# VectorE's order inside the delta pairs: convolution taps of v into its waits, masked attention ahead of level one

## What is computed

```python
qkv = silu(causal_dwconv(concatenate([dq, dk_, dv_]), dn_conv_w))      # 4 taps per channel
cq, ck = l2norm(cq), l2norm(ck)
G = cumsum(g);  L = where(causal, exp(G[:, None] - G[None, :]), 0)
A = where(strict, einsum('id,jd->ij', k_beta, kc) * L, 0)
sol = triangular_solve(eye + A, [v * beta, k_beta * exp(G)])           # u, w
attn = where(causal, einsum('id,jd->ij', qc, kc) * L, 0)
# then over the chunks:
v_new = u - w @ S;  o = q_dec @ S + attn @ v_new;  S = S * d + k_dec.T @ v_new
```

## Time and profile before

| | us |
|---|---|
| median of 3 runs | 2281.53 (2281.12 to 2284.86) |
| the profiled execution's own time | 2283.54 |
| its span | 2281.8 |
| TensorE busy, matmuls | 2227.6 (98%) |
| VectorE busy | 1076.5 (47%) |
| ScalarE busy | 801.2 (35%) |
| GpSimd busy | 943.0 (41%) |

### The profile page before, as it was taken

One profiled execution on the slowest core, in us unless ns is written; L12 is line 12 of the kernel. 1 busy time (PEld: TensorE's weight loads), 2 busy tenths in 40 slices (PEclk: granted clock), 3 DMA queues, 4 the chain that ended last, 5 costly groups with the idle time before them and its releaser, 6 DMA issues.

```text
span 2281.8 us, 30104 instructions
## 1 busy us (share of the span) xinstructions
PE 2227.6 (98%) x12106; PEld 1794.7 (79%) x12106; DVE 1076.5 (47%) x1508; ACT 801.2 (35%) x825; POOL 943.0 (41%) x509
## 2 busy tenths in 40 slices
PE   7999999999999999999999999999999999999998
PEld 6888888776656888888887888787878778888887
DVE  5423203775854343331063532646556545888801
ACT  4222213447644342222143532332424243322213
POOL 4555544343312445554443244323233343444344
PEclk9999999999999999999999999999999999999999
DMA  4233223343332333223232123212121243322232
GB/s 151 93 93 106 87 99 95 89 70 56 78 101 94 98 105 92 92 92 101 92 103 93 56 70 95 77 56 75 56 75 56 75 148 109 94 92 92 73 101 83
DMA packets 162169, 203.36 MB, mean 89 GB/s; under 512 B 12236, under 2 KB 117015, under 8 KB 162071
## 3 DMA queue, kind: packets, MB, share of 16 engines
q1 hardware_dynamic: 155296, 197.16, 28.5%
q10 hardware_dynamic: 6775, 4.80, 0.7%
HBM read 191.45 MB, written 10.49 MB: 88 GB/s over the span
## 4 chain that ended last, share of the span: by engine, by line
PE 83%; DVE 7%; issue 5%; ACT 3%; POOL 1%; DMA 0%; ACTq 0%; POOLq 0%; DVEq 0%
PE PS L213 23%; PE PS L215 22%; PE PS L214 22%; PE PS L244 2%; PE PS L246 2%; PE PS L245 2%; DVE cv L2350 2%; POOL wl L204 1%; PE PS L1134 1%; PE PS L2159 1%; PE PS L1674 1%; PE PS L1231 1%; PE PS L2176 1%; DVE work L2428 1%; PE PS L1050 0%
## 5 line engine op out<-in xcount | busy, mean ns | idle before, releaser
L204 POOL TENSOR_TENSOR wl<-raw,wh 128x1024 fp32r<-128x1024 f32 x335 | 864.0, 2594 | 1233.7 <-ACT wh L193 1195.9
L213 PE MATMUL PS<-h_hi,wh 128*128 128x512 f32 x1696 | 678.8, 400 | 7.9 <-ACT stage_a L863 3.0
L215 PE MATMUL PS<-h_hi,wl 128*128 128x512 f32 x1696 | 663.3, 391 | 0.0
L214 PE MATMUL PS<-h_lo,wh 128*128 128x512 f32 x1696 | 662.9, 391 | 0.0
L193 ACT ACTIVATE wh<-raw 128x2048 fp32r<-128x2048 f32 (+1 forms) x214 | 332.6, 1554 | 837.8 <-PE PS L215 791.7
L213 PEld LDWEIGHTS PS<-h_hi,wh 128*128 128x128 f32 x1696 | 319.5, 188 | 92.1 <-issue 20.3
L215 PEld LDWEIGHTS PS<-h_hi,wl 128*128 128x128 f32 x1696 | 319.6, 188 | 67.8
L214 PEld LDWEIGHTS PS<-h_lo,wh 128*128 128x128 f32 x1696 | 319.9, 189 | 61.8 <-issue 0.7
L213 PE MATMUL PS<-act_hi,wh 128*128 (+1 forms) x528 | 205.8, 390 | 1.0 <-POOL wl L204 1.0
L694 DVE SCALAR_TENSOR_TENSOR xT<-PS,xT 128x512 f32<-128x512 f32 x40 | 27.2, 689 | 379.6 <-PE PS L215 379.5
L214 PE MATMUL PS<-act_lo,wh 128*128 (+1 forms) x528 | 205.5, 389 | 0.0
(11 more groups left out here) (450 smaller groups left out, 2842.0 us busy)
## 6 DMA issues: line engine op xcount, KB each, us to landing
raw<-in_w_in_dram SPq DMA_DIRECT2D x94, 512.0 KB, 4.6
raw<-in_w_up_dram SPq DMA_DIRECT2D x82, 512.0 KB, 4.7
raw<-in_w_down_dram SPq DMA_DIRECT2D x132, 256.0 KB, 2.7
raw<-in_w_gate_dram SPq DMA_DIRECT2D x42, 512.0 KB, 3.9
raw<-in_w_in_dram SPq DMA_DIRECT2D x20, 256.0 KB, 3.7
raw<-in_w_out_dram SPq DMA_DIRECT2D x16, 256.0 KB, 2.9
raw<-in_w_ret_br_dram SPq DMA_DIRECT2D x8, 512.0 KB, 4.3
gates<-stage SPq DMA_DIRECT2D x16, 256.0 KB, 5.9
```

The source lines that it names most:

```text
L204: ins = nc.gpsimd.tensor_tensor(wl[:, slot, part], raw[:, slot, part], wh[:, slot, part].bitcast(F32), ALU.subtract)
L213: nc.tensor.matmul(dst, sh, mh, start=start, stop=False)
L214: nc.tensor.matmul(dst, sh, ml, start=False, stop=False)
L215: return nc.tensor.matmul(dst, sl, mh, start=False, stop=stop)
```

## The change

Only `delta_dve` changes. v's taps 0 and 1 go ahead of the wait for eR (behind a new wait for cin), tap 2 between the clipping and the product that makes A, tap 3 stays behind A. The factor `rk` goes ahead of the start blocks, the two instructions of the masked attention go from level one to right behind the start blocks, ahead of the memset and the scaled v. No instruction is added or removed, and the other engines' programs stay as they were.

```diff
                      "dve")
+            v_taps = conv_taps(dve, pp, 4, 6, cin)
+            await_point(dve, "act", pp, "cin")
+            v_taps[0]()
+            v_taps[1]()
             await_point(dve, "act", pp, "eR")
             dve_link(tt(chunks(wE), chunks(PS[:, 4:6, :]), per_head(Gn, pp), ALU.subtract))
             at_point(dve.tensor_scalar(wE, wE, 0.0, None, ALU.max), "dve")
+            v_taps[2]()
             await_point(dve, "pe", pp, "kk")
             await_point(dve, "act", pp, "eE")
...
-            v_taps = conv_taps(dve, pp, 4, 6, cin)
-            for tap in v_taps:
-                tap()
+            v_taps[3]()
+            await_point(dve, "act", pp, "rk")
+            rk3 = rk.rearrange("p (e c) -> p e c", e=2)
+            dve_link(tt(rk3, rk3, beta[:, :, 2 * pp:2 * pp + 2].rearrange("p c h -> p h c"), ALU.mult))
             start_block(Tc, wU, level[1], lambda r: r)
             await_point(dve, "act", pp, "AT")
             at_point(start_block(Uc, wAT[:, :, :], level1T, other), "dve")
+            dve_link(tt(tiles(wE), tiles(wE), everywhere(seen), ALU.mult))
+            tt(wE, PS[:, 0:2, :], wE, ALU.mult).then_inc(attn_set, 1)
             dve.memset(quarters(wU, 64, 0), 0.0)
-            await_point(dve, "act", pp, "rk")
-            rk3 = rk.rearrange("p (e c) -> p e c", e=2)
-            dve_link(tt(rk3, rk3, beta[:, :, 2 * pp:2 * pp + 2].rearrange("p c h -> p h c"), ALU.mult))
             scaled_v(dve, pp, 6)
...
-                if l == 0:
-                    dve_link(tt(tiles(wE), tiles(wE), everywhere(seen), ALU.mult))
-                    tt(wE, PS[:, 0:2, :], wE, ALU.mult).then_inc(attn_set, 1)
```

## The result

| | before | after |
|---|---|---|
| median | 2281.89 (2281.12 to 2284.86) | 2257.52 (2256.78 to 2259.0) |
| profiled execution, its span | 2283.54, 2281.8 | 2256.78, 2255.1 |
| mean granted clock | 0.992 | 0.998 |

The change is faster by 24.4 us between the medians; the ratio is 0.9892, 95% interval 0.9875 to 0.9909. That is 1.1% of the time, and the two sets of runs do not overlap. A second set on another occasion gave 2256.86 against 2281.57.

What follows compares the result with a forecast made beforehand. TensorE, its matmuls filling 98% of the span, was taken as the bound, so only its waits and half clock could be won. 3.6 + 3.05 = 6.65 a pair (6.95 with the race won); 6.75 x 4 = 27.0, giving 2254.5, range 2249 to 2265.

Steps and rivals of the forecast that it cites:

- Taps 0 and 1: VectorE's idle 3.09 before eR: the two taps, 2.35 together, fit in and cost nothing, with 0.7 left.
- Tap 2: Gap of 1.20 on VectorE before A: the tap needs 1.42, so A comes 0.24 later, +0.24.
- v's SiLU and GpSimd's weights: TensorE's waits ahead of level one: -0.47 from earlier SiLU, -0.62 from GpSimd's weights; X starts 0.85 earlier, at 1562.65.
- VectorE's chain to the first mask: VectorE's new order, with holds by GpSimd: first mask at 1564.3 against 1564.78 if GpSimd is first at the last add.
- Level one: Correction 0.65 after the mask, at 1564.95; second level's X at 1566.9 instead of 1570.48, 3.6 earlier.
- The prediction's sign of being wrong: A stretch at 0.50 clock remaining in each pair, or level one's masks starting 2 us after its X is there.
- Clock, -3.05: Granted clock 1.00 throughout: level two 2.1 shorter, level three 0.95, together -3.05 a pair; bounds 0 and 3.4.
- the race at the last add: VectorE's last add meets GpSimd's L204: second level's X 3.6 earlier if GpSimd is first, 3.9 if VectorE wins.
- Rival 1: Clock falls all the same, on level one's short gaps and small matmuls: saving 14.4 alone, 2267; chance 8%.
- Rival 2: One more GpSimd hold, 2.25, between tap 3 and level one's mask: mask at 1566.55, saving 17.6, 2264; chance 6%.
- Rival 3: Attention ahead of the first mask only shifts the stall from level two to level one, clock falling there: 2282; chance 2%.
- Rival 4: Taps slow by their form, 2.82 wherever they stand: A 5.9 late, clock falls, +9.3, 2291; chance 4%.

Runs made afterwards that it cites:

- The filled gap: Kernel before, with 24 matmuls that nothing needs put into TensorE's wait between level one's corrections and level two: 2271.49 us, ratio 0.9957.
- attention_alone: Kernel before, with only the masked attention moved, ahead of the memset; taps and factor in their old places: 2283.16 us, ratio 1.0008.
- factor_back: The change, with the 128x8 factor back in its old place behind the memset: 2257.41 us, ratio 0.9894.
- x_early: The change, with TensorE's wait for ScalarE's copy of the fourth gates' product moved from ahead of level one's X to behind it: 2257.84 us.
- mask_early: The change, with the masked attention's product with PSUM moved into level two and the memset into level three, behind the masks: 2257.38 us.
- factor_alone: Kernel before, with only the 128x8 factor moved, ahead of v's taps: 2263.03 us, ratio 0.9921.
- both_early: The change with X not waiting for ScalarE's copy and the PSUM product and memset moved behind later masks: 2254.82 us; second set 2254.58 against 2256.86.

## Why the prediction was right, and where it was off

The range and the side held: 2254.5 forecast, 2257.5 measured. Of the 3.0 between them 1.5 lie in the stage that the sum is about, 1.1 between the stage and the medians, and 0.4 in the median before (2281.53 of three runs then, 2281.89 of four now). By the prediction's own steps:

- **Taps 0 and 1 cost nothing**: right. They took 2.3 and left VectorE 0.92 idle before eR; 0.7 was said.
- **Tap 2, +0.24**: right. The wait for A went from 0.23 to 0.47.
- **v's SiLU and GpSimd's weights, -0.47 and -0.62**: both waits are gone, but X came only 0.88 earlier from A, where 1.09 was worked out (0.85 plus A's 0.24). Of the 0.21 missing, 0.17 is in v's transposes: with TensorE waiting ahead of them (before) their loads start within 0.82 from the first to the next matmul's, directly behind the product (after) 0.99. A wait that goes does not give back all of what it showed.
- **VectorE's chain to the first mask**: from A's transposes the prediction has T0 at +14.3 and the mask at 1564.3 - 1543.84 = +20.5; measured +14.4 (1547.55 + 2.87 - 1536.04) and +20.77. Each hold that the text names is there, in its order, and so is GpSimd's won race. This step bore the most reasoning and missed by 0.3: the PSUM product, the memset and the scaled v take 3.05 from the end of seen to the mask, where 2.79 was added up.
- **Level one**: X to X 4.19, 4.25 worked out, and here two errors cancel. The prediction let the correction follow the mask by 0.65, read from a level in which X and not the mask set the correction (1.97 behind X). Where the mask sets it, it follows in 0.47 (1556.81 to 1557.28). So the mask's 0.3 of lateness cost only 0.1. The prediction's sign of being wrong, masks 2 us behind X, was not far: they start 1.75 behind it.
- **Clock, -3.05**: levels two and three 2.13 and 0.83 shorter, 2.96 together, the second of them 0.12 less than the 0.95 said. That 0.95 was not what its own terms give: 0.78 for X and 0.1 for the matmuls behind it are 0.88. The filled gap gives 2.96 by itself.

Together 6.41 a pair by A to A (102.68 against 109.09, the third pair 102.79) against the 6.75 of the sum; over the stage 25.5, not 27.0. Of the 0.34 a pair that is missing, the start of X is 0.21, of which level one gave 0.06 back, the clock 0.09, and 0.1 was weight that the 6.75 put on VectorE winning the race at the last add, which it lost. The profiled executions differ by 26.8 only because 1.4 of it lies ahead of the first changed instruction (below). Against that the medians' 24.4 is 1.1 below the stage's own gain; 0.7 of it is that the profiled execution after was the fastest of its four. The outcome of the race at the last add, 0.05 us, was not something that the prediction could call; it had priced both.

Rival 1, the clock swinging on short gaps alone, is out: of the kernels tried, only `attention_alone`, which keeps the long gap, falls to half clock in the pairs; the others have the short gaps and 1.00. In the pairs, gaps of 0.36 to 1.5 never came with a fall, and gaps of 3.4 and 4.2 did in the traces kept. The Trainium skill (TensorE: Matmul & The Clock Gate, "A second HAM failure mode: psum-queue depth-cycling") tells of micro-idles between groups of matmuls that were frequent enough to make the clock swing, in another kernel, of bf16 matmuls with 512 columns; in this one the short gaps were not enough. The 3.4 may not lower the clock every time: of 35 runs of the kernel before that stand beside these experiments and the result, four took 2276.1 to 2279.1 at a mean clock of 0.994 to 0.995. At 2.96 us for each stretch at half clock that would be one or two of them missing (an estimate; no trace of such a run was kept). Rival 2, one more hold ahead of the mask, did not come: TensorE waited 0.25 longer for the mask than its shortest gap, not the 2.6 of that case (its mask at 1566.55 and 0.65 behind it, against 1564.62). Rival 3, the gap that moves whole, is what `attention_alone` measures, with the taps and the factor left in their old places. Rival 4 fell with the taps at 0.75 in every form.

What the prediction did not see, though its rows held it, is how little of the change was needed. It read the stall as attention standing in the wrong level. But 2.1 of the 3.33 of seen was time held by GpSimd's operation (unheld it takes 1.22), in a race lost by 0.11 us. Once VectorE waits for level one's X and not the other way round, seen starts 0.4 earlier against GpSimd and wins, and two quite different edits reach that: the change with the attention taken back (2259.3), or one 128x8 instruction moved (2263.0). The gap fell from 3.42 to 0.89 and the half clock went with it, on an order of arrival. Beside the kernel before, the factor alone gave 18.5, taps and factor 22.8, all three moves 24.4; given the taps and the attention's new place, the factor's place gave nothing (`factor_back`). No run moves the taps alone.

## What to carry to other kernels

Where VectorE instructions with two SBUF operands come out two or four times as long as the same form elsewhere, look at GpSimd's timeline before looking at the instruction: what is priced may be GpSimd's operation. Here the 128x8 instruction paid 2.2 us of it and the 128x1024 one 2.1; moved out of that stretch, or started 0.4 us earlier, each was free of it. A stall of TensorE of some microseconds should be priced with the half clock behind it, here 3.0 us on top of 3.1. And of two engines that both reach a meeting point late, shortening either alone can give nothing (`x_early`) or little (`mask_early`); try the two edits together before dropping them.

## What was not expected

- The 128x8 factor takes 2.37 when held and 0.17 at its shortest (`factor_alone`; 0.38 in `factor_back`). As a filler between GpSimd's two operations it delays them little: the two take 5.06 with the factor between them, 5.51 with a 64x512 mask (`factor_back`) and 4.70 with nothing. The two places of the factor measured the same time.
- With less waiting some pairs lengthen, most often the third, in level two. In `mask_early` its corrections and panel take 2.74 from the first load to the next X, against 1.95 in the second pair. No wait on another engine is longer than the usual one; TensorE pauses in the middle of the corrections, for nothing that the profile shows:

```profile
1664.25 0.14 PEld L2176 LDWEIGHTS PS<-work 64*64 64x64 f32 x2 [0.36 <-DVE work L2429]
...
1665.39 0.13 PEld L2176 LDWEIGHTS PS<-work 64*64 64x64 f32 x1 [0.60 <-issue]
...
1666.99 0.31 PEld L2159 LDWEIGHTS PS<-work,w_AT 64*64 64x64 f32 x8 [0.36 <-DVE work L2440]
```

  The change itself shows 0.1 to 0.2 of this in its third pair, `both_early` 0.4 and, run again, 1.4; `factor_alone` shows it in its first and fourth. It eats part of what the faster versions win. No run here tells its cause.
- The start of the program differs from run to run. The profiled execution before had a stretch at half clock at 18.70 that the one after had not, and reached the first pair's A later by the 1.4 named above (1434.51 against 1433.36, and the A of after has its own 0.24 on top). The stretches, first before, then after:

```profile
18.70:21.90 3.20, 3.20 (x9) 2.48 (x8) 3.20 (x3) 1.17 (x2) 3.20 (x2) 0.50 0.93 316
```

```profile
18.70:21.90 3.20, 3.20 (x16) 2.63 (x15) 3.20 (x4) 1.48 (x3) 2.88 (x2) 1.00 0.91 311
```

  Ahead of them stand two gaps of different length, first before, then after. That fits the gaps of the pairs: 1.97 with no fall behind it, 2.99 with one.

```profile
17.52 0.19 PEld L213 LDWEIGHTS PS<-h_hi,wh 128*128 128x128 f32 x1 [2.99 <-POOL wl L204]
```

```profile
17.63 0.19 PEld L213 LDWEIGHTS PS<-h_hi,wh 128*128 128x128 f32 x1 [1.97 <-POOL wl L204]
```
